# Three more sevenfold products in each of two feed-forward parts, with merged joins, in a transformer kernel on one core

## What is computed

```python
# first block
gate = h2 @ w_gate; up = h2 @ w_up
x = x + (silu(gate) * up) @ w_down            # 1024 -> 2816 -> 1024
# second block, twice
def conv_ffn(h, w_up, conv_w, conv_b, w_down):
    u = h @ w_up                              # 1024 -> 2 * 2816
    c = causal depthwise conv of u, 3 taps, + conv_b
    g, val = split(c, 2)
    return (silu(g) * val) @ w_down           # 2816 -> 1024
```

## Time and profile before

| | |
|---|---|
| time of the launch, median of 3 runs | 1713.11 us (1712.53 to 1713.64) |
| the profiled execution's own time | 1712.91 us |
| its span on the core | 1711.1 us |
| TensorE busy | 1700.8 us (99%), clock 0.999 of full |
| VectorE busy | 1278.1 us (75%) |
| ScalarE busy | 864.3 us (51%) |
| GpSimd busy | 361.6 us (21%) |
| down the chain that ended last | TensorE 94%, VectorE 4% |

### The profile page before, as it was taken

One profiled execution on the slowest core, in us unless ns is written; L12 is line 12 of the kernel. 1 busy time (PEld: TensorE's weight loads), 2 busy tenths in 40 slices (PEclk: granted clock), 3 DMA queues, 4 the chain that ended last, 5 costly groups with the idle time before them and its releaser, 6 DMA issues.

```text
span 1711.1 us, 24883 instructions
## 1 busy us (share of the span) xinstructions
PE 1700.8 (99%) x9596; PEld 1476.2 (86%) x9596; DVE 1278.1 (75%) x1968; ACT 864.3 (51%) x1530; POOL 361.6 (21%) x264
## 2 busy tenths in 40 slices
PE   9999999999999999999999999999999999999998
PEld 8888888998998888888888988889898888898897
DVE  5789656897696846695979966755889687996575
ACT  5554533443354646554545533547877454454354
POOL 2003204442325011102144202022110213520200
PEclk9999999999999999999999999999999999999999
DMA  5212333334222221213233341323111234334122
GB/s 173 74 62 72 99 99 124 99 99 146 77 75 87 62 82 57 73 51 98 88 134 111 99 123 50 90 74 93 40 50 50 87 95 127 99 99 136 62 87 74
DMA packets 125196, 152.90 MB, mean 89 GB/s; under 512 B 7526, under 2 KB 96904, under 8 KB 125080
## 3 DMA queue, kind: packets, MB, share of 16 engines
q1 hardware_dynamic: 124776, 150.99, 27.9%
q10 hardware_dynamic: 304, 0.33, 0.1%
HBM read 148.61 MB, written 2.10 MB: 88 GB/s over the span
## 4 chain that ended last, share of the span: by engine, by line
PE 94%; DVE 4%; POOL 1%; issue 1%; ACT 1%; DVEq 0%; ACTq 0%; POOLq 0%
PE bk L2422 23%; PE bk L2424 23%; PE bk L2423 23%; PE bk L2464 5%; PE bk L2466 5%; PE bk L2465 5%; PE bk L2427 4%; PE bk L2569 2%; DVE FS L2624 1%; POOL FS L3011 1%; PE bk L2603 1%; PE bk L2530 1%; PE bk L2602 1%; DVE WL L2636 1%; PE bk L2557 1%
## 5 line engine op out<-in xcount | busy, mean ns | idle before, releaser
L2422 PE MATMUL bk<-R,WH 128*128 128x512 f32 (+1 forms) x1394 | 521.2, 374 | 0.9 <-DVE WL L2636 0.7
L2424 PE MATMUL bk<-R,WL 128*128 128x512 f32 (+1 forms) x1394 | 515.0, 369 | 0.0
L2423 PE MATMUL bk<-R,WH 128*128 128x512 f32 (+1 forms) x1394 | 514.8, 369 | 0.0
L2636 DVE TENSOR_TENSOR WL<-RAW,WH 128x1024 fp32r<-128x1024 f32 (+5 forms) x198 | 248.2, 1255 | 153.5 <-ACT WH L2861 152.3
L2861 ACT ACTIVATE WH<-RAW 128x1024 fp32r<-128x1024 f32 (+5 forms) x198 | 202.8, 1026 | 213.8 <-PE bk L2424 152.5
L2422 PEld LDWEIGHTS bk<-R,WH 128*128 128x128 f32 x1394 | 263.0, 189 | 45.3 <-DVE WL L2636 2.1
L2424 PEld LDWEIGHTS bk<-R,WL 128*128 128x128 f32 x1394 | 262.8, 189 | 44.9
L2423 PEld LDWEIGHTS bk<-R,WH 128*128 128x128 f32 x1394 | 263.2, 189 | 41.0
L3007 POOL TENSOR_TENSOR OVER<-TOK 128x1024 f32<-128x1024 f32 x28 | 76.3, 2725 | 382.0 <-DVE WL L2633 216.4
L2464 PE MATMUL bk<-WH,R 128*128 128x512 f32 (+4 forms) x394 | 144.7, 367 | 0.0
L2466 PE MATMUL bk<-WL,R 128*128 128x512 f32 (+4 forms) x394 | 139.3, 353 | 0.0
(11 more groups left out here) (235 smaller groups left out, 3251.8 us busy)
## 6 DMA issues: line engine op xcount, KB each, us to landing
RAW<-in_ffn_w_down_dram SPq DMA_DIRECT2D x44, 512.0 KB, 3.9
RAW<-in_ffn_w_up_dram SPq DMA_DIRECT2D x64, 256.0 KB, 3.0
TOK<-in_ffn_w_up_dram SPq DMA_DIRECT2D x14, 1024.0 KB, 5.1
RAW<-in_ffn_w_up_dram SPq DMA_DIRECT2D x28, 512.0 KB, 3.6
RAW<-in_w_down_dram SPq DMA_DIRECT2D x22, 512.0 KB, 3.6
RAW<-in_da_w_qkv_dram SPq DMA_DIRECT2D x32, 256.0 KB, 3.0
TOK<-in_w_gate_dram SPq DMA_DIRECT2D x7, 1024.0 KB, 5.4
TOK<-in_w_up_dram SPq DMA_DIRECT2D x7, 1024.0 KB, 5.0
```

Of the source, the lines that this page charges most:

```text
L2422: e.matmul(dst, lh, rh, start=start, stop=False)
L2423: e.matmul(dst, lh, rl, start=False, stop=False)
L2424: return e.matmul(dst, ll, rh, start=False, stop=stop)
L2636: e.tensor_tensor(low, sides(st.n, raw_home(st.n)), high.bitcast(F32), ALU.subtract).then_inc(on["wlo_dve"], 1)
```

## The change

In each of the two convolution parts the up halves of blocks 4, 6 and 8 become units as well, so that a part has ten units in place of seven. The joins of every unit, those of the first block's part too, are merged: the seven products now take five PSUM banks (two products share a bank, side by side, twice), and three joins of 512 elements and one of 256 take the place of seven of 256; one more `keep` on ScalarE copies an intermediate result from one FS slot to the other, between the second and the third join. The sums of activations in `Combined.make` go to a pair of scratch rows in the TOK buffers (`PART`) in place of two FS slots, and the four steps follow one another, since each waits until the one before has split its last sum. The planner's rules change too: VectorE steps that read two SBUF operands and the GpSimd steps `wsum` and `xsum` are planned in turn, never side by side; `tap1`, `tap0` and `prod` are now among them; and the cost of `wsum` is lower.

```diff
-PARTS = (range(0, 4), range(4, 8), range(8, 11))
-SEVENS = ({fb: (0, 2) for fb in range(4, 11)}, {fb: (0,) for fb in range(4, 11)}, {fb: (0,) for fb in range(4, 11)})
+THIRDS = (range(0, 4), range(4, 8), range(8, 11))
+BLOCKS = (THIRDS, THIRDS, THIRDS)
+SEVENS = ({fb: (0, 2) for fb in range(4, 11)}, {fb: (0, 2) if fb in (4,6,8) else (0,) for fb in range(4, 11)}, {fb: (0, 2) if fb in (4,6,8) else (0,) for fb in range(4, 11)})
...
+EARLY = -2
+MARGIN = (3, 5, 5)
+RANKS = (1.5, 0.5)
...
-SBUF_ONLY = ("wlo", "lo", "p_one", "p_two", "kv_scale")
+SBUF_ONLY = ("wlo", "lo", "p_one", "p_two", "kv_scale", "tap1", "tap0", "prod")
+POOL_READS = ("wsum", "xsum")
...
-        return 300.0 + 2.7 * width_of(f["dst"])
+        return 100.0 + 2.25 * width_of(f["dst"])
...
+                    shares = eng == "pool" and kind in POOL_READS or eng == "dve" and kind in SBUF_ONLY and not from_bank(fields)
+                    if shares:
+                        since, until = shared["dve" if eng == "pool" else "pool"]
+                        if since <= t < until:
+                            t = until
...
-                while kp and self.own[kp - 1] is None:
+                while kp and (self.own[kp - 1] is None or ("s4", kp - 1) not in self.of):
...
-                e, o, p, q = slots = [fsl.get() for _ in range(4)]
-                E, O, A, B = (FS[:, s.i, 0:S] for s in slots)
+                e, o = fsl.get(), fsl.get()
+                E, O = (FS[:, s.i, 0:S] for s in (e, o))
+                A, B = PART
...
-            b, done = yield from product(n1, 1, "a12")
...
+            b2, _ = yield from product(n1, 1, "a12")
...
-            b6, done6 = yield from product(n4, 0, "s2")
+            _, done6 = yield from product(n4, 0, "s2", b2, 256)
...
+                st = yield step("join", dst=FS[:, l.i:r.i + 1:r.i - l.i, 0:256], src=halves_of(b2), x=one.unsqueeze(1).to_broadcast([P, 2, 256]),
+                                op=ALU.add, after=counts([done6, q.first, l.free, r.free]))
...
+                third = yield step("join", dst=right[:, 256:S], src=BK[b7.i][:, 0:256], x=right[:, 0:256], op=ALU.add, after=counts([done7, st.dve]))
...
+                copied = yield step("keep", dst=FS[:, l.i, 256:S], src=right[:, 256:S], after=counts([third.dve, l.free]))
+                st = yield step("join", dst=right.rearrange("p (x c) -> p x c", x=2), src=BK[b5.i][:, 0:256].unsqueeze(1).to_broadcast([P, 2, 256]),
+                                x=right.rearrange("p (x c) -> p x c", x=2), op=ALU.subtract, after=counts([done5, third.dve, copied.act]))
...
+                st = yield step("join", dst=both, src=halves_of(b4), x=both, op=ALU.add, after=counts([done3, q.low]))
```

More of the change, by code:

```diff
@@ L204, in takes @@
             return dve(n) if f["scale"] is None else 1.45 * dve(n) if f["from_x"] else 1.1 * dve(n)
[L205 removed]
+        if kind in ("max", "join"):
             return dve(width_of(f["src"]))
@@ L502, in plan_ffn @@
                 zones[layer] = [len(chunks), len(chunks), len(units)]
-            for fb in PARTS[part]:
+            parts = BLOCKS[layer]
+            for fb in parts[part]:
                 sevenfold = SEVENS[layer].get(fb, ())
@@ L534, in build @@
         plan_rows(w_out, 512, 4)
-        for part in range(len(PARTS)):
+        for part in range(len(BLOCKS[0])):
             plan_ffn(part, ((w_gate, 0), (w_up, 0)), w_down)
@@ L546, in build @@
         plan_last_rows(da_o, 768)
-        for part in range(len(PARTS)):
+        for part in range(len(BLOCKS[1])):
             plan_ffn(part, ((up2[0], 0), (up2[0], 2816)), dn2[0])
@@ L1700, in seven @@
             q = Group()
-            q.first = q.second = q.third = q.left = q.right = q.y = None
-            one, two = PART[u % 2][:, 0:256], PART[u % 2][:, 256:S]
+            q.first = q.low = q.both = None
+            one = PART[u % 2][:, 0:256]
             def split(n):
@@ L1708, in split, with product @@
                 return w_low[n].dve
-            def product(n, half, name):
-                b = yield from bank("gemm")
-                st = yield step("piece", n=n, half=half, xs=X.operand(name), bank=b.i, after=counts([w_low[n].dve, X.ready, b.free]))
+            def product(n, half, name, b=None, o=0):
+                if b is None:
+                    b = yield from bank("gemm")
+                st = yield step("piece", n=n, half=half, xs=X.operand(name), bank=b.i, o=o, after=counts([w_low[n].dve, X.ready, b.free]))
                 if half or n == n2:
@@ L1723, in seven, with first @@
             yield from split(n1)
[L1724 to L1728, removed]
+            b1, done1 = yield from product(n1, 0, "a11")
+            def first():
+                st = yield step("keep", dst=one, src=BK[b1.i][:, 0:256], after=counts([done1, part_free[u % 2]]))
+                put_bank(b1, st.act)
                 q.first = st.act
-            spawn(first(b, done), 0)
-            b, done = yield from product(n1, 1, "a12")
[L1734 to L1742, removed]
+            spawn(first(), 0)
+            b2, _ = yield from product(n1, 1, "a12")
             yield from split(n3)
@@ L1746, in seven @@
             yield from split(n4)
-            b6, done6 = yield from product(n4, 0, "s2")
+            _, done6 = yield from product(n4, 0, "s2", b2, 256)
             def middle():
-                while q.first is None:
+                while q.first is None or len(fsl.fr) < 2:
                     yield None
-                q.second = yield from join(two, b6, done6, one, ALU.add, q.first, part_free[u % 2])
-                put_bank(b6, q.second)
-                while q.left is None:
-                    yield None
[L1756 to L1777, removed]
```

108 lines of the change are left out of this document (66 added, 42 removed).

## The result

The changed kernel takes 1718.05 us, median of 11 runs (1715.64 to 1719.31), beside 1713.11 us before: a ratio of 1.0028, with a 95% interval of 1.0019 to 1.0037. It is slower by 4.9 us where 4.6 us less were forecast, and the time lies outside the range. The profiled execution took 1718.11 us, with a span of 1716.3 us.

What follows compares the result with a forecast made beforehand. TensorE, busy 1700.8 of 1711.1 us, was taken as the bound. From the profiled 1712.9 us, 5.0 us less on TensorE and 0.4 us of new waits gave 1708.3, plus 0.2 for the median: 1708.5 us, range 1707.0 to 1713.0.

Steps and rivals of the forecast that it cites:

- TensorE, -5.0 us: In the convolution parts, six plain halves become units, each 0.84 us shorter on TensorE: 5.0 us less.
- VectorE's amount: Each added unit costs VectorE 4.3 to 6.05 us, each old unit gains 0.46 us; just enough time or 3.6 us short.
- The new copies on ScalarE: One more copy a unit, 0.37 us, hidden by ScalarE and taken at nothing; at the other end 1.0 us a unit.
- The start of a unit stretch: Before the first unit, the successive activation-sum steps end between 907.9 and 913.5 us, before 916.2: no cost.
- VectorE may trail that far: VectorE's surplus of up to 3.6 us runs on into the down projection, since it trails 13 us now without TensorE waiting.
- The term of 0.4 us for new waits: New TensorE waits lie between 0 and 3.6 us; 0.4 us taken, the longest wait of that kind before.
- the first rival: VectorE's surplus is not carried over, adding 3.6 us of TensorE waits: 1711.7 us; chance 0.17 together with a smaller gain.
- The shared path to SBUF: Rival: GpSimd's added sums stop VectorE's two-SBUF-operand instructions, giving 20.8 us of TensorE waits, 1728.9 us; chance 0.09.

Runs made afterwards that it cites:

- e10: The kernel before with two added units in each convolution part (blocks 4 and 8) and nothing else of the change: 1709.64 us, ratio 0.998.
- e5: The changed kernel with ScalarE's last block copy, VectorE's split of it and GpSimd's second-unit sums held back until the activations are made: 1712.32 us.
- e9: e5 with weight splits ahead of all other ready VectorE work within a unit stretch while fewer than four blocks are in stock: 1709.89 us, ratio 0.9981.
- e1: The changed kernel with only VectorE's split of the first unit's last weight block moved behind all activation splits of that unit: 1716.8 us.
- e2: The changed kernel with the list of units of the kernel before, so merged joins, serial make steps and new planner without added units: 1720.3 us.
- e7: The changed kernel with the make steps of the kernel before; joins, added units and planner stay: 1714.72 us.

## Why the prediction was wrong

**TensorE, -5.0 us: right.** e10's 3.4 us for four units agree with 0.84 us a unit, and blocks 8 and 9, with one added unit, take 41.14 us where they took 41.96.

**VectorE's amount: near.** In the window of blocks 4 to 7 of the first part (914.4 to 999.2 us) it is busy 79.6 us, and the prediction gave 78.9 to 82.4. But part of that work runs in the down projection behind it. From block 4's first matmul to block 8's VectorE is busy 103.0 us, before 92.0: 11.0 us more, where the prediction's own difference is 6.8 to 10.3. The merged join takes 0.68 us, as taken from the nearest row. The new copies on ScalarE, taken at nothing, show no cost either: the first block's part, with fourteen units, is 0.4 us shorter.

**"The start of a unit stretch. Cost: nothing": the step that failed.** It added up how long three make steps take by themselves and found them done between 907.9 and 913.5 us. It did not ask in which place of each queue their parts stand. VectorE's timeline before has the last activation splits ahead of the first unit's weight splits, done 6 us before the unit begins at 916.2; after, the scalings that begin the second and the fourth step read (first fence: before; second: after):

```profile
907.33 3.03 DVE L2650 TENSOR_TENSOR R<-FS,R 128x512 fp32r<-128x512 f32 x4
910.29 1.21 DVE L2633 TENSOR_TENSOR KT<-OVER,KT 128x1024 fp32r<-128x1024 f32 x1
```
```profile
877.75 3.60 DVE L2635 SCALAR_TENSOR_TENSOR FS<-XT,VEC,FS 128x512 f32<-128x512 f32 x2
...
903.71 1.41 DVE L2635 SCALAR_TENSOR_TENSOR FS<-XT,VEC,FS 128x512 f32<-128x512 f32 x2
```

So the second and third step together took 26.0 us, where the prediction has 15.8 to 19.4: each waits for the last split of the one before, and that split stands behind other work of VectorE. (The second step's last sum is ready at 887.8; its split begins at 891.73.) The weight splits of the first unit now stand ahead of the last activation splits. The last of these ended at 917.34: behind a copy that waited 4.38 us for a weight slot on ScalarE, behind 2.69 us of the same wait on VectorE, and then beside GpSimd's sums. The document even showed the weight sum moved ahead of the last activation sum and counted it as 3.25 us of GpSimd's time, not as time in which VectorE's splits stand still. In place of nothing the start cost 5.2 us of TensorE's time and 2.9 us of falls of the clock. e5 takes both away; its time falls by 5.7 us only, since blocks 4 to 7 lose more there.

**"VectorE may trail that far": half right.** It can trail into the down projection, as e9 shows, but not by itself: the weight splits of the block's plain half stand behind taps and joins, and TensorE needs them at once. The term of 0.4 us for new waits measured 3.3 us in the changed kernel (1.5 and 1.8 us in blocks 4 to 7 of the two parts), and 5.3 us in e5. This is the first rival, near its price of 3.6 us and above it in e5. Even without the failed step the time would have been that of e5, 1712.3 us: 3.8 us above the forecast, inside the range.

**The shared path to SBUF** did not stop the added units for whole sums, but it is there. Groups of VectorE after, 914.4 to 999.2 us (count, busy, mean ns, idle before):

```profile
L2644 DVE TENSOR_TENSOR KT<-OVER,KT 128x1024 fp32r<-128x1024 f32 x6 | 12.6, 2096 | 4.6 <-ACT KT L2870 4.6
...
L2635 DVE SCALAR_TENSOR_TENSOR FS<-FS,VEC 128x510 f32<-128x510 f32 x10 | 8.0, 844 | 0.0
L2635 DVE SCALAR_TENSOR_TENSOR FS<-FS,VEC 128x511 f32<-128x511 f32 x10 | 8.0, 844 | 0.0
```

Taps out of FS take 844 ns on average, where they took 1275 and 1088: the new plan's order holds most of them apart from the sums. Splits into KT of the sums take 2096 ns, where a split of that size takes 1212. The stall moved from the taps to them.

## What to carry to other kernels

When a plan is reordered, look at the head of every queue where a stage begins: an instruction that is early by the planner's clock and waits for a slot holds back everything behind it, on each engine that touches the same data. A fix on one engine alone shows little (e1: 0.6 us a wait) as long as another queue has the same order. When TensorE stands idle, look at the granted clock of the matmuls behind the wait too: here a fall cost 1.4 to 1.5 us on top of a wait of 2.9. And see which work of a saturated engine TensorE asks for first, before calling the rest carried over.

## Not expected of the hardware

In the first part a wait of 2.9 us of TensorE was followed, after 1.5 us at the full clock, by 3.4 us at 1.2 GHz (0.213 us in place of 0.120 us a matmul of 256 columns). In the second part the slow matmuls begin within 0.4 us of the wait's end:

```profile
1482.57 0.55 PE L2433 MATMUL bk<-PT,KT 128*128 128x256 f32 x1 [2.92 <-DVE R L2661]
1482.91 0.42 PE L2434 MATMUL bk<-PT,KT 128*128 128x256 f32 x1
```

Nor is a fall certain: in e2 the same wait of 2.9 us had a fall behind it in the first part (granted clock 0.54 from 920 to 923) and none in the second, and in e1 one of the two waits of 2.3 us had one. Behind e7's waits of 1.6 us none was seen. The runs of e1 lie in three groups to match: three near 1715.1 (mean granted clock 0.999 to 1.0), five near 1716.9 and three near 1718.2 us (0.997). What decides between them stays open.
